# Hybrid decoder trunk, two layers: four projection chunks go from fp32 products to split halves, with the low halves formed on VectorE

## What is computed

```
h = rms_norm(x, norm_g)
proj = einsum('bsd,de->bse', h, w_in)
u_lru, u_s5, qkv_ret, q_nsa, kv_nsa, bg_nsa, gate_paths, merge = split_columns(proj, IN_SIZES)
...
ys = ys * silu(gate_paths)
branch = einsum('bsnw,nwd->bsnd', ys, w_branch)
merged = sum(sigmoid(merge) * branch, axis=2)
x = x + einsum('bsd,de->bse', merged, w_out)
```

## Time and profile before

| | |
|---|---|
| median of 3 runs | 883.88 us (882.99 to 884.66) |
| the profiled execution, its own time | 883.38 us |
| its span, first to last instruction | 881.6 us |
| mean granted TensorE clock | 0.973 |
| busy: PE, DVE, ACT, POOL | 824.0, 562.3, 312.9, 313.7 us |

### The profile page before, as it was taken

One profiled execution on the slowest core, in us unless ns is written; L12 is line 12 of the kernel. 1 busy time (PEld: TensorE's weight loads), 2 busy tenths in 40 slices (PEclk: granted clock), 3 DMA queues, 4 the chain that ended last, 5 costly groups with the idle time before them and its releaser, 6 DMA issues. The chain is left out here.

```text
span 881.6 us, 10702 instructions
## 1 busy us (share of the span) xinstructions
PE 824.0 (93%) x3852; PEld 608.4 (69%) x3852; DVE 562.3 (64%) x937; ACT 312.9 (35%) x519; POOL 313.7 (36%) x134
## 2 busy tenths in 40 slices
PE   4999989999999799999879998999998989999995
PEld 3874764446878688888768556744477777888884
DVE  3888999464697652634268889964928974445342
ACT  5310212013743445464334112110164544555441
POOL 0000000005568576668400000000057676666872
PEclk9999999999999899999979999999999998999998
DMA  7575524445345444454255745344453344444551
GB/s 227 135 240 152 184 84 140 122 146 189 116 120 168 120 143 144 144 168 147 69 113 150 236 137 191 96 143 128 136 190 122 117 140 127 138 137 154 168 167 71
DMA packets 87507, 128.29 MB, mean 146 GB/s; under 512 B 22204, under 2 KB 32792, under 8 KB 87320
## 3 DMA queue, kind: packets, MB, share of 16 engines
q1 hardware_dynamic: 87448, 127.55, 46.5%
HBM read 126.48 MB, written 1.05 MB: 145 GB/s over the span
## 5 line engine op out<-in xcount | busy, mean ns | idle before, releaser
L560 POOL TENSOR_TENSOR w_lo<-raw,w_hi 128x1024 fp32r<-128x1024 f32 x120 | 307.0, 2588 | 534.1 <-ACT w_hi L576 503.1
L1371 PE MATMUL proj<-raw,h_full 128*128 128x512 f32 (+1 forms) x512 | 213.2, 572 | 0.0
L1371 PEld LDWEIGHTS proj<-raw,h_full 128*128 128x128 f32 x512 | 95.7, 190 | 104.5 <-issue 100.6
L576 ACT ACTIVATE w_hi<-raw 128x1024 fp32r<-128x1024 f32 x120 | 122.5, 1050 | 65.1 <-DMA raw<-in_s_w_glu 27.1
L1327 PE MATMUL proj<-w_hi,h_hi 128*128 128x512 f32 x320 | 128.7, 402 | 0.9 <-POOL w_lo L560 0.9
L1367 PE MATMUL proj<-h_full,raw 128*128 128x256 f32 x512 | 119.0, 393 | 7.5 <-DVE gate L978 7.5
L1327 PE MATMUL proj<-w_lo,h_hi 128*128 128x512 f32 x320 | 125.0, 391 | 0.0
L1327 PE MATMUL proj<-w_hi,h_lo 128*128 128x512 f32 x320 | 125.0, 391 | 0.0
L1367 PEld LDWEIGHTS proj<-h_full,raw 128*128 128x128 f32 x512 | 100.2, 198 | 23.1 <-DVE gate L978 7.9
L1327 PEld LDWEIGHTS proj<-w_hi,h_hi 128*128 128x128 f32 x320 | 60.1, 188 | 14.3 <-issue 1.7
L1327 PEld LDWEIGHTS proj<-w_hi,h_lo 128*128 128x128 f32 x320 | 60.1, 188 | 13.0
(11 more groups left out here) (283 smaller groups left out, 1194.6 us busy)
## 6 DMA issues: line engine op xcount, KB each, us to landing
raw<-in_w_in SPq DMA_DIRECT2D x154, 512.0 KB, 3.5
raw<-in_w_branch SPq DMA_DIRECT2D x32, 512.0 KB, 3.6
raw<-in_w_out SPq DMA_DIRECT2D x16, 512.0 KB, 3.7
raw<-in_s_w_glu SPq DMA_DIRECT2D x8, 512.0 KB, 3.6
raw<-in_w_in SPq DMA_DIRECT2D x8, 256.0 KB, 2.5
merged<-in_nsa_ck_w SPq DMA_DIRECT2D x4, 512.0 KB, 5.7
mt<-in_nsa_ck_w SPq DMA_DIRECT2D x4, 512.0 KB, 6.8
merged<-in_nsa_cv_w SPq DMA_DIRECT2D x4, 512.0 KB, 5.1
```

Of the source, the lines that this page charges most:

```text
L560: nc.gpsimd.tensor_tensor(w_lo[:, s % N_SPLIT, 0:n * w], raw[:, u % N_RAW, 0:n * w], w_hi[:, s % N_SPLIT, 0:n * w].bitcast(f32), ALU.subtr ...
L576: i = nc.scalar.activation(out_, in_, func, **kw)
L1371: last = mm(ps[:, 512 * t:512 * t + w], h_full[:, k, t * P:(t + 1) * P], rw, start=st_, stop=sp_, skip_group_check=True)
```

## The change

Four chunks, merge_s5_1, ret_q, ret_k and nsa_q, leave the list of native chunks and become split. Their low halves are not formed on POOL: POOL skips them, and DVE does them, at places written into its queue, with a signal of its own (vlo_done). ACT casts their high halves; its look-ahead at merge_s5_0 is set to two units, and it casts the rest of merge_s5_1 ahead of trig(7). PE and SP wait through a helper for the signal of the engine that made the low half. The low half of a unit of these chunks also frees its raw buffer.

```diff
-NATIVE = (... "merge_s5_0", "merge_s5_1", "ret_q", "ret_k", "nsa_q")
+NATIVE = (... "merge_s5_0")
...
+LO_ON_VECTOR = ("merge_s5_1", "ret_q", "ret_k", "nsa_q")
+VECTOR_UNITS = [u for u in SPLIT_UNITS if CHUNKS[UNITS[u][0]][0] in LO_ON_VECTOR]
...
+        def wait_low(eng, u):
+            if u in VECTOR_UNITS:
+                eng.wait_ge(vlo_done, vector_splits(u + 1))
+            else:
+                eng.wait_ge(lo_done, splits(u + 1) - vector_splits(u + 1))
...
                         if u - N_RAW in SPLIT_UNITS:
-                            sp.wait_ge(lo_done, splits(u - N_RAW + 1))
+                            wait_low(sp, u - N_RAW)
...
                             u = SPLIT_UNITS[s]
                             c, _, n, w = UNITS[u]
+                            if u in VECTOR_UNITS:
+                                continue
                             gp.wait_ge(hi_done, s + 1)
...
-                    def next_cast(name):
-                        cast_units(min(NU, UNIT_END[CHUNK[name]] + N_SPLIT - 1))
+                    def next_cast(name, ahead=N_SPLIT - 1):
+                        cast_units(min(NU, UNIT_END[CHUNK[name]] + ahead))
...
-                        next_cast(full)
+                        next_cast(full, 2 if full == "merge_s5_0" else N_SPLIT - 1)
...
                     run(hid_q, hid_q, ACT.Tanh, hid_tanh, scale=GELU_C)
+                    cast_units(UNIT_END[CHUNK["merge_s5_1"]])
                     trig(7)
...
+                    def split_lo(name, *which):
+                        for n in which:
+                            u = UNIT_END[CHUNK[name] - 1] + n
+                            s = splits(u)
+                            dve.wait_ge(hi_done, s + 1)
+                            if s >= N_SPLIT:
+                                wait_unit_read(dve, SPLIT_UNITS[s - N_SPLIT])
+                            v.tensor_tensor(w_lo[:, s % N_SPLIT, :], raw[:, u % N_RAW, :],
+                                            w_hi[:, s % N_SPLIT, :].bitcast(f32), ALU.subtract).then_inc(vlo_done, 1)
...
                     angles(7)
+                    split_lo("merge_s5_1", 0, 1)
                     scan_pair(6)
...
+                    split_lo("merge_s5_1", 2, 3)
+                    split_lo("ret_q", 0)
                     scan_pair(7)
+                    split_lo("ret_q", 1, 2, 3)
+                    split_lo("ret_k", 0, 1, 2)
                     s5_out(3)
...
                     v.tensor_tensor(gelu_t, gelu_t, yf, ALU.mult).then_inc(z_arg, 1)
+                    split_lo("ret_k", 3)
                     rope_ret(0, "ret_q")
+                    split_lo("nsa_q", 0)
                     dve.wait_ge(z_tanh, 1)
...
                     v.tensor_tensor(yf, yf, gelu_t, ALU.mult).then_inc(z_ready, 1)
+                    split_lo("nsa_q", 1)
                     dve.wait_ge(z_hi, 1)
                     v.tensor_tensor(flat(ys_lo[:, :, :]), yf, ..., ALU.subtract).then_inc(z_lo, 1)
+                    split_lo("nsa_q", 2, 3)
...
-                                pe.wait_ge(lo_done, splits(u + 1))
+                                wait_low(pe, u)
```

More of the change, by code:

```diff
@@ L67, with vector_splits @@
 N_SPLIT = 5
-NATIVE = ("u_s5", "cmp", "u_lru", "ret_v", "nsa_kv", "gate_s5", "gate_lru", "merge_s5_0", "merge_s5_1", "ret_q", "ret_k", "nsa_q")
+NATIVE = ("u_s5", "cmp", "u_lru", "ret_v", "nsa_kv", "gate_s5", "gate_lru", "merge_s5_0")
 SPLIT_UNITS = [u for u in range(NU) if CHUNKS[UNITS[u][0]][0] not in NATIVE]
+LO_ON_VECTOR = ("merge_s5_1", "ret_q", "ret_k", "nsa_q")
+VECTOR_UNITS = [u for u in SPLIT_UNITS if CHUNKS[UNITS[u][0]][0] in LO_ON_VECTOR]
 def splits(upto):
     return sum(u < upto for u in SPLIT_UNITS)
+def vector_splits(upto):
+    return sum(u < upto for u in VECTOR_UNITS)
 V_NORM, V_CONV, V_CONVB, V_BA, V_BX, V_LAM, V_D, V_BGLU, V_LR, V_LI, V_DT, V_ROWS = (
@@ L272, in hybrid_trunk @@
         raw_loaded = [sem(f"raw_loaded{i}") for i in range(N_RAW)]
-        hi_done, lo_done, unit_used = sem("hi_done"), sem("lo_done"), sem("unit_used")
+        hi_done, lo_done, vlo_done, unit_used = sem("hi_done"), sem("lo_done"), sem("vlo_done"), sem("unit_used")
         chunk_done = sem("chunk_done")
@@ L542, in _ @@
                     for u in range(N_FIRST):
-                        sp.wait_ge(lo_done, splits(max(w for w in range(NU) if w % N_RAW == u) + 1))
+                        wait_low(sp, max(w for w in range(NU) if w % N_RAW == u))
                         load_unit(sp, u, (l + 1) % DEPTH, nxt["raw_first"])
```

## The result

The changed kernel takes 896.93 us (median of 4 runs, 896.6 to 899.36) against 884.27 us before (4 runs). The ratio is 1.0151, with a 95% interval of 1.0129 to 1.0173: 13 us slower. The profiled execution has a span of 894.9 us, 13.3 more than before, and the mean granted clock fell from 0.973 to 0.958.

What follows compares the result with a forecast made beforehand. The prediction took PE's queue of matmuls to bound the kernel; waits for DVE, POOL's delay of the convolution and lost clock came to 7.8 us a layer net, taking 883.4 to 899.0 us, range 888 to 906.

Steps and rivals of the forecast that it cites:

- What PE saves: Four chunks in two layers: 11.06 us each instead of 13.93, saving 22.9 us in all if nothing waits.
- Step 1: merge_s5_1: scan_pair(6) starts later, and PE idles 2.4 us, from 158.1 to 160.5, for DVE's subtraction of unit 2.
- Step 2: ret_q: PE waits 2.4 us or more for unit 1, subtracted after scan_pair(7); state_outputs(7) ends at 185.0, against 182.6.
- Half clock after each: Sign to look for: PE at half clock after its idle times in merge_s5_1, ret_q and ahead of the RG-LRU matmuls.
- Step 3: s5_out(3) to the convolution: DVE's added subtractions and a cast wait move the convolution's start from 194.26 to 202.1.
- Step 4: Convolution: POOL wakes at about 202, its five units delay DVE's small operations, and xc_ready comes at 219.0.
- Step 5: Behind the convolution: PE waits 208.1 to 219.0, RG-LRU matmuls take 6.4 us at half clock; 7.8 us lost a layer.
- Sum: Whole kernel: both layers lose 7.8 us each, taking the profiled 883.4 us to 899.0 us.
- A: Rival: the convolution isn't held up by POOL; a layer gains 6 us, giving 871 us; chance 6%.
- B: Rival: DVE hides all of its added work and the full saving comes through, 860 us; chance 2%.
- C: Rival: early losses hold, but POOL's units come with pauses; 1 to 3 us late a layer, 886 to 889 us; chance 14%.

Runs made afterwards that it cites:

- e1: The changed kernel, with POOL waiting for xc_ready, the end of the convolution, before its first low half of a layer: 881.63 us, ratio 0.9979.
- e7: The changed kernel with the moved subtractions of e5, but without POOL's wait of e1: 884.14 us, ratio 0.9997.
- e8: The kernel before the change, with eight extra 128x1024 subtractions on POOL from the start of the convolution: 914.0 us, ratio 1.0329.
- e5: e1 with three DVE subtractions (merge_s5_1 unit 1, ret_q units 1 and 2) moved into scan_pair(6) and scan_pair(7): 865.91 us, ratio 0.9789.

## Why the prediction held, point by point

- **What PE saves** held: ret_k and nsa_q take 11.2 and 11.1 us in the changed kernel.
- **Step 1** held: an idle time of 2.24 us for 2.4, and the half clock behind it (0.70 over 3.4 us in layer 0). In layer 1 an idle time of the same length (2.25 us) cost nothing, the clock stayed at 1.00.
- **Step 2** is the first term that was mis-sized. The wait in ret_q was 2.10 us in layer 0 and the clock stayed full behind it, so state_outputs(7) ended at 183.0 and not at 185.0. In layer 1 the wait was 3.71 us and the clock 0.50 over 4.5 us. I had charged 1.7 us for the clock to both; it was about 0 and 2.3. "Half clock after each", one of the signs that I had named, so held for one of the two short waits in each layer: behind the first in layer 0, behind the second in layer 1.
- **Step 3** held: 17.2 us from s5_out(3) to the convolution, predicted 17.1.
- **Step 4** held, and it carries the result: POOL's first unit at 200.12 (about 202), five in 11.97 us (12.2), the convolution 16.6 us (16.9), PE's wait 11.09 us (10.9). That POOL and the convolution both began 2 us early left their overlap as forecast: DVE's last subtraction ahead of the convolution and POOL's first one both wait for the casts that ACT does from 198.04 on. e1 and e7 take it away and put it back, e8 makes it in the kernel before. The price from the earlier trace rows, one DVE operation for each POOL unit, was the right one.
- **Step 5**: the RG-LRU matmuls took 6.6 us at half clock (6.4), and branch_s5_0 ran at full clock, starting 5.7 us late where I had 7.8; the 2 us are those of step 2. The transposes behind it waited 2.04 us in both layers. In layer 0 the clock fell behind that, to 0.66 over 4.9 us: about 1.7 us lost, where I had put 0.4 for wait and clock. In layer 1 it stayed at 1.00. So in layer 0 this second mis-sized term stands against the first one: part of the 2 us that step 2 had too much is made up by it, and the sum is so far closer by luck.
- **Sum**: layer 0 became 6.2 us longer (the first transposes of layer 1 start at 453.25 instead of 447.08) and layer 1 7.1 us, 13.3 against the 15.6 forecast; 896.9 against 899.0 us.

Of the rivals, A needed POOL's first unit after 207 (it came at 200.12), B ret_q unit 1 subtracted by 168 (it was subtracted from 172.26), and C pauses between POOL's units (there were none). e5 arranges what A and B asked for, and comes out between their two times, at 865.9 us.

## What to carry to other kernels

When work leaves an engine's way, look at what it releases: here split chunks free their load buffers early, the next chunk's data arrives early, and GpSimd wakes up in the middle of the small VectorE operations that everything waits for. A GpSimd instruction of 2.4 us costs VectorE a whole turn for an operation of 0.34 us that reads SBUF alone, so hold the long ones back until a run of short ones is over; one wait was worth 15 to 18 us. And work put into an in-order queue should stand where its first reader needs it, if necessary in the middle of a longer step: the same subtractions at other places were worth another 13 to 16 us.

## What the runs showed of the hardware that was not expected

Operations that read PSUM and one SBUF tensor were not delayed at all (0.69 us at 207.44 in e1, with POOL busy since 207.00). A tensor_scalar with a single SBUF input takes turns with POOL just as operations with two do: the one on eight columns in the earlier trace rows had said so, and here four of 128x256 took 9.63 us instead of 1.38. And a short idle time of PE doesn't always cost clock: after 2.24 us it fell in layer 0, after 2.25 us in layer 1 it didn't; what decides it stays open. The twelve single runs of e1 spread over 6.7 us, where the five of e5, which has fewer waits of 2 us and more, spread over 1.5 us; that the clock is the cause of the spread was not tested.
